# Modulation rows of chunks 4 to 17 as weighted sums on VectorE, in the two projection stages, stored by accumulating transfers

## Chip, cores and metric

The kernel runs on one core of a Trainium2 chip. The metric is the device time of one launch in microseconds; less is better. Five engines work side by side and wait for each other through semaphores: TensorE (PE: matmuls and transposes into PSUM), VectorE (DVE), ScalarE (ACT), GpSimd (POOL; here it only issues transfers) and SyncE (SP; it issues transfers too). All data are float32.

## What is computed

Two transformer-like blocks run one after the other on 512 tokens of width 1024. Each block turns a conditioning vector into rows of shift, scale and gate, the modulation:

```python
# first block
mod = jnp.einsum('bd,de->be', jax.nn.silu(c), w_ada[l]) + b_ada[l]         # 3 x 1024
shift, scale, gate = jnp.split(mod, 3, axis=-1)
h = rms_norm(x, norm_pre[l]) * (1.0 + scale[:, None, :]) + shift[:, None, :]
proj = jnp.einsum('bsd,de->bse', h, w_in[l])
...   # recurrence (RG-LRU), dilated attention, output projection
x = x + gate[:, None, :] * rms_norm(mix, norm_post[l])
# second block
mod = (s_lat @ w_ada[l] + b_ada[l]).reshape(B, N_MOD, 1, D)                # 6 x 1024, latent
mod_c = (s_ctx @ w_ada[l] + b_ada[l]).reshape(N_MOD, 1, 1, D)              # 6 x 1024, context
p_l = modulate(x, norm1_g[l], mod[:, 0], mod[:, 1]) @ w_in[l]
p_c = modulate(ctx, norm1_g[l], mod_c[0], mod_c[1]) @ w_in[l]
...   # pooling, differential attention, RWKV scan, merge, mixture of experts
```

The two weight matrices `w_ada` are cut into 18 chunks of 1024 x 512 (2 MB each): chunks 0 to 5 belong to the first block (0 to 3 are shift and scale, 4 and 5 the gate), 6 to 17 to the second. Chunks 6 to 9 (shift and scale of the second block) are wanted for the latent and for the context vector, chunks 10 to 17 only for the latent one.

## The kernel before

The kernel is written engine by engine: each stage has one function for each engine (`proj1_tensor`, `proj1_vector`, ...), and each engine runs its functions in a fixed order. A wait names the event it needs (`T[...]` from TensorE, `V[...]` from VectorE, `d_...[...]` for a transfer); everything behind it on the same engine waits too. Nothing is reordered at run time. VectorE waits for its own last instruction before each new one.

The stages that matter here, with their place in the trace: the start with the modulation of chunks 0 to 3 (0 to 37 us); the **first projections** (`PROJ1`, 24 tiles of eight 128x512 matmul steps, 37 to 222 us), with the recurrence in them; **attention** (`att_...`, 35 steps over 4 query blocks i and 8 heads h, key width 128(i+1), 222 to 310 us); the **output projection** of the first block (`out1_...`, 8 mix tiles, then norms and transposes, 310 to 391 us); the **second projections** (`TILES2`: pool 0-3, q 0-3, kc/k 0-3 in turn, v 0-5; 391 to 545 us); then differential attention, third projections, the scan, the merge, and from about 1400 us the experts, whose weights stream in.

In attention one step x does on TensorE, in this order: scores of step x+1, transposes of the probabilities of step x-2, a third of a modulation chunk (`ada_tensor`), and the product with V of step x-3. VectorE does bias and row maximum, ScalarE the exponential and the copy of the transposes.

A modulation chunk j from 4 on is computed by `modulation_blocks`: 8 slices k times 4 column groups t, 32 matmuls of `cs[:, k, :]` (128x32, three of its columns hold the vectors) against 128 columns of the weights. `ADA` cuts each chunk into steps of 12, 12 and 8 matmuls; 35 steps stand in the attention loop and the 36th behind it; chunks 16 and 17 stand at the end of `out1_tensor`. `ada_vector(j)` adds the bias and writes `mrow`, and `ada_gpsimd(j)` stores the row to DRAM (`mods1`, `mods2`), from where later stages fetch it. The chunks come through the three 4096-column weight buffers (`MAIN_CHUNKS`, `W`), loaded by SP in one fixed order with all other weights; a load waits until the chunk three places before it is used up. So weight chunk 26, the first of the second projections, waits for chunk 13, the last of the output projection.

`Late` runs short generators beside a row of tiles: each `add` or `step` moves each pending one forward. In the second projections a q or k tile is squared (ACT), summed (`bs` matmul, behind the next tile), rooted (ACT), and on VectorE inverted and scaled (a reciprocal and a `stt`, a scalar_tensor_tensor), then rotated (`rot2` matmul, one more tile later, and three tensor_tensor).

## Time and profile before

| | us |
|---|---|
| median of 3 runs | 1870.52 (1866.34 to 1871.33) |
| span of the profiled execution | 1876.8 |
| TensorE busy | 1717.6 (92%) |
| VectorE busy | 804.7 (43%) |
| ScalarE busy | 518.8 (28%) |
| GpSimd busy | 109.4 (6%) |
| attention, 221.0 to 309.6 | 88.6 |
| output projection with its end, 309.6 to 391.4 | 81.8 |

The page gives the span as the execution's only time; it is 6.3 us above the median of the three timed runs. The row of slices on the page shows TensorE at 9 tenths or more in nearly all of the first 33 of 40 slices, and the DMA row at 9 only from slice 30 on, in the experts. In a timeline row the columns are start, duration, engine, line, operation, destination and source, shapes and count; in brackets stands the idle time before it and what ended it. TensorE's durations of merged rows run from the first start to the last end, and neighbouring rows overlap a little.

### The profile page before, as it was taken

The page shows a single profiled execution, that of the slowest core. Times are in us where ns is not written, and L with a number is a line of the kernel's source. Part 1 is how long each engine was busy: PE and PEld are TensorE (multiplying, and loading weights), DVE is VectorE, ACT ScalarE, POOL GpSimd, SP SyncE. Part 2 cuts the span into 40 slices and gives each one's busy share as a digit, 9 for nine tenths or more (in the row PEclk, how much of TensorE's full clock was granted, in tenths as well). Part 3 has the DMA queues.
Part 4 walks back from the last instruction along what each step waited for, and adds up shares of the span by engine and source line. Part 5 has one row for each costly group of instructions (what it writes and reads, how often), then busy time and mean ns, then how long its engine had stood idle before and what let it go on. Part 6 is the DMA issues. An engine that isn't in the chain of part 4 may idle for free.

```text
span 1876.8 us, 37887 instructions
## 1 busy us (share of the span) xinstructions
PE 1717.6 (92%) x16822; PEld 927.4 (49%) x16822; DVE 804.7 (43%) x1484; ACT 518.8 (28%) x983; POOL 109.4 (6%) x144
## 2 busy tenths in 40 slices
PE   5999999999999999999999999999999977778786
PEld 3444566544546555556667667544454333323332
DVE  3853144656627456355654554344462211222210
ACT  3710254311127422354453341122231110101010
POOL 0000010010000000100000000000001101010100
PEclk8999989999989999999998998899999999999998
DMA  9121376351110030042221210356569999999997
GB/s 396 76 88 47 145 287 247 145 224 69 45 45 1 23 151 0 17 170 82 77 81 50 63 56 24 114 219 221 219 239 398 416 425 415 422 413 425 417 423 279
DMA packets 48360, 359.25 MB, mean 191 GB/s; under 512 B 8325, under 2 KB 8557, under 8 KB 28736
## 3 DMA queue, kind: packets, MB, share of 16 engines
q1 hardware_dynamic: 35792, 311.51, 41.2%
q0 software_dynamic: 12400, 45.27, 7.3%
q8 instruction: 134, 2.20, 0.5%
q14 instruction: 34, 0.28, 0.0%
...
## 4 chain that ended last, share of the span: by engine, by line
PE 74%; DMA 16%; ACT 4%; issue 3%; DVE 2%; POOL 0%; SPq 0%; ACTq 0%; DVEq 0%; POOLq 0%
PE psum L207 71%; DMA arena<-in_w 16%; PE psum L210 3%; ACT arena L204 3%; ACT L204 1%; DVE arena L154 1%; DVE arena L180 0%; DVE arena L164 0%; DVE arena L172 0%; DVE arena L160 0%; POOL arena L141 0%; DMA arena<-in_tok 0%; DVE arena L168 0%; DVE arena L159 0%; POOL out L149 0%
## 5 line engine op out<-in xcount | busy, mean ns | idle before, releaser
L207 PE MATMUL psum<-arena 32*32 32x16 f32 (+12 forms) x16178 | 1638.1, 304 | 145.2 <-DMA arena<-in_w 73.4
L207 PEld LDWEIGHTS psum<-arena 32*32 32x32 f32 (+5 forms) x16178 | 856.0, 135 | 876.3 <-issue 764.7
L204 ACT ACTIVATE arena<-psum 128x512 f32<-128x512 f32 (+5 forms) x334 | 171.4, 513 | 871.2 <-PE psum L207 670.7
L154 DVE TENSOR_TENSOR arena<-arena,psum 128x512 f32<-128x512 f32 (+3 forms) x128 | 64.9, 507 | 402.6 <-PE psum L207 209.2
L154 DVE TENSOR_TENSOR arena<-arena 128x512 f32<-128x512 f32 (+10 forms) x315 | 191.6, 608 | 31.0 <-ACT arena L204 14.7
L204 ACT ACTIVATE arena<-arena 128x512 f32<-128x512 f32 (+10 forms) x254 | 138.8, 546 | 177.7 <-DVE arena L154 41.9
L204 ACT ACTIVATE arena<-psum,arena 128x128 f32<-128x128 f32 (+3 forms) x221 | 111.7, 505 | 275.1 <-PE psum L210 135.5
L154 DVE TENSOR_TENSOR arena<-psum,arena 128x128 f32<-128x128 f32 (+3 forms) x116 | 47.4, 409 | 154.5 <-PE psum L207 141.3
L164 DVE SCALAR_TENSOR_TENSOR arena<-arena 128x512 f32<-128x512 f32 (+7 forms) x162 | 103.5, 639 | 14.5 <-ACT arena L204 8.1
L210 PE MATMUL psum<-arena 128*128 128x128 f32 x644 | 102.6, 291 | 6.1 <-ACT arena L204 3.2
L172 DVE RECIPROCAL arena<-arena 128x1 f32<-128x1 f32 (+4 forms) x71 | 79.1, 1113 | 63.0 <-ACT arena L204 59.2
L210 PEld LDWEIGHTS psum<-arena 128*128 128x128 f32 x644 | 73.6, 146 | 64.3 <-issue 46.0
L164 DVE SCALAR_TENSOR_TENSOR arena<-psum,arena 128x512 f32<-128x512 f32 (+4 forms) x84 | 49.6, 591 | 114.8 <-PE psum L207 111.2
L204 ACT ACT_TABLE_LOAD x68 | 87.2, 1283 | 18.8 <-DMA arena<-gd 11.6
L159 DVE TENSOR_SCALAR arena<-arena 128x32 f32<-128x32 f32 (+10 forms) x126 | 39.8, 316 | 57.7 <-ACT arena L204 52.7
L184 DVE COPY_PREDICATED arena<-arena,psum 128x512 f32<-128x512 uint32 (+1 forms) x60 | 35.9, 598 | 45.4 <-PE psum L207 41.3
L168 DVE COPY arena<-psum 128x512 f32<-128x512 f32 (+4 forms) x53 | 27.8, 525 | 63.2 <-PE psum L210 35.4
L180 DVE TENSOR_REDUCE arena<-psum 128x1 f32<-128x768 f32 x32 | 30.6, 958 | 47.8 <-PE psum L207 46.0
L149 POOL DMA_INDIRECT out<-arena x16 | 25.1, 1566 | 408.6 <-DVE arena L164 139.5
L143 POOL DMA_DIRECT2D arena<-kd x28 | 21.1, 753 | 240.9 <-DVE arena L154 135.3
L143 POOL DMA_DIRECT2D mods<-arena x26 | 14.4, 557 | 312.4 <-DVE arena L154 304.2
L160 DVE TENSOR_SCALAR arena<-psum,arena 128x128 f32<-128x128 f32 x64 | 26.2, 410 | 8.5 <-PE psum L210 5.0
...
## 6 DMA issues: line engine op xcount, KB each, us to landing
...
kd<-arena POOLq DMA_DIRECT2D x2, 1536.0 KB, 11.0
```

Of the source, the lines that this page charges most:

```text
L143: self.e.dma_start(out, in_).then_inc(*signal)
L154: return self.ends(self.e.tensor_tensor(out, a, b, op))
L159: return self.ends(self.e.tensor_scalar(out, a, s1, None, op0))
L160: return self.ends(self.e.tensor_scalar(out, a, s1, s2, op0, op1))
L164: return self.ends(self.e.scalar_tensor_tensor(out=out, in0=a, scalar=s, in1=b, op0=op0, op1=op1))
L168: return self.ends(self.e.tensor_copy(out, a))
L172: return self.ends(self.e.reciprocal(out, a))
L180: return self.ends(self.e.tensor_reduce(out, a, AX, op, negate=negate))
L184: return self.ends(self.e.copy_predicated(out, mask, a))
L204: return self.ends(self.e.activation(out, a, func, **kw))
L207: return self.ends(self.e.matmul(out, lhs, rhs, start=start, stop=stop))
L210: return self.ends(self.e.transpose(out, a, ident))
```

## The change

Chunks 4 to 17 are no longer multiplied on TensorE slice by slice. VectorE forms for each chunk and vector the weighted sum over the 8 slices (each slice 128x512 times a per-partition scalar of `cs`, one `tensor_scalar` and seven `scalar_tensor_tensor`), and TensorE then only sums over partitions: 4 matmuls against a 128x32 matrix with a column of ones (`one_column`), for chunks 6 to 9 twice 4. The bias is not added any more: `mods1` and `mods2` are filled with the bias by two DRAM to DRAM transfers, and the rows are added to them by accumulating transfers.

The weights of these chunks leave the three big buffers. They come in 56 quarters ("parts") of 128x1024 (0.5 MB) into two small buffers (`ada_in`), issued by GpSimd; the load of part n waits until VectorE is done with part n-2. Parts 0 to 23 (chunks 4 to 9) are summed in the first projections, parts 24 to 55 (chunks 10 to 17) in the second. In the attention loop only the 8 matmuls of chunk 9 are left, and in `out1` none. `MAIN_CHUNKS` gets 14 entries shorter, so weight chunk 26 now waits for chunk 11 instead of 13. VectorE's copy `ada_vector(j)` (128x128) and the store stay, spread over the same stages. SP waits for the last store before it loads the first expert chunk, GpSimd before the third projections.

```diff
-MAIN_CHUNKS = [0, 1, 2, 3, 6, 7, 8, 9, 10, 11, 4, 5, *range(14, 24), 12, 13, 24, 25, *range(26, 34), *range(40, 45)]
+MAIN_CHUNKS = [0, 1, 2, 3, 6, 7, 8, 9, 10, 11, 12, 13, *range(26, 34), *range(40, 45)]
...
+                if ("p1", t) in ADA_SUMS:
+                    ada_tensor(ADA_SUMS["p1", t], ALL8)
...
+        ADA_VECTORS = {j: (0,) if j < 6 else (1, 2) if j < 10 else (1,) for j in ADA}
+        ADA_SUMS = {("p1", 12): 4, ("p1", 13): 5, ("p1", 18): 6, ("p1", 20): 7, ("p1", 22): 8, ("att", 2): 9, ("q", 0): 10, ("q", 1): 11,
+                    ("k", 0): 12, ("kc", 2): 13, ("v", 0): 14, ("v", 1): 15, ("v", 3): 16, ("v", 4): 17}
...
+                     ("v", 0): (44, 47), ("v", 1): (47, 50), ("v", 2): (50, 53), ("v", 3): (53, 56)}.items()}
...
+        def ada_load(n):
+
+            j, q = 4 + n // 4, n % 4
+            if n > 1:
+                G.wait_ge(ada_by(n - 2)["part", n - 2])
+            G.dma(ada_in[n % 2].rearrange("p k n -> p (k n)"), T_["w"][ada_chunk(j), :, 1024 * q:1024 * q + 1024], d_aw[n % 2].up(n))
+
+        def ada_part_vector(n):
+
+            j, q = 4 + n // 4, n % 4
+            V.wait_ge(d_aw[n % 2][n])
+            for v in ADA_VECTORS[j]:
+                s = ada_at(j, v)
+                if q == 0 and s > 3:
+                    V.wait_ge(T["ada", ADA_SLOTS[s - 4][0]])
+                for k in range(2):
+                    w, by = ada_in[n % 2][:, k, :], cs[:, 2 * q + k, v:v + 1]
+                    if q == 0 and k == 0:
+                        V.ts(ada_sum[s % 4], w, by, None, ALU.mult)
+                    else:
+                        V.stt(ada_sum[s % 4], w, by, ada_sum[s % 4], ALU.mult, ALU.add)
+            V.then_inc("part", n)
+
+        def ada_tensor(j, ring):
+            T.wait_ge(ada_by(4 * j - 13)["part", 4 * j - 13], *ps.take(ring, "ada", j))
+            last = ADA_VECTORS[j][-1]
+            for v in ADA_VECTORS[j]:
+                for t in range(4):
+                    T.mm(ps["ada", j][32 * t:32 * t + 32, 0:128], one_column(v), ada_sum[ada_at(j, v) % 4][:, c4(t)],
+                         v == ADA_VECTORS[j][0], v == last)
+            T.then_inc("ada", j)
...
-                ada_tensor(*next(steps), MBANK)
+                if ("att", x) in ADA_SUMS:
+                    ada_tensor(ADA_SUMS["att", x], MBANK)
...
+                if before[n, m] in ADA_SUMS:
+                    ada_vector(ADA_SUMS[before[n, m]])
+                for part in ADA_PARTS.get((n, m), ()):
+                    ada_part_vector(part)
...
+            Y.wait_ge(*mods_stored(17))
             Y.dma(EB0, T_["w"][45], WE.count((0, 0)).up("w", (0, 0)))
...
-            G.wait_ge(*end3())
+            G.wait_ge(*end3(), *mods_stored(17))
```

How the change stands in three places. The first is TensorE in attention, at steps with key width 128 and 256 (128x256 and 128x128 on L207 are scores, L210 is the transpose, 128x64 the product with V, 32x128 the modulation). Before:

```order
L207 MATMUL psum<-arena 128x256
L210 MATMUL psum<-arena 128x128 [waits s_dve]
L207 MATMUL psum<-arena 32x128 x8
L207 MATMUL psum<-arena 128x64 [waits s_act]
L207 MATMUL psum<-arena 128x256
L210 MATMUL psum<-arena 128x128 [waits s_dve]
```

And now, from step 2 on (lines are three higher in the changed file):

```order
L213 MATMUL psum<-arena 128x128 [waits s_act]
L210 MATMUL psum<-arena 32x128 x8
L210 MATMUL psum<-arena 128x128 [waits s_dve]
L213 MATMUL psum<-arena 128x128 [waits s_dve,s_act]
L210 MATMUL psum<-arena 128x64 [waits s_act]
L210 MATMUL psum<-arena 128x128 [waits s_dve]
L213 MATMUL psum<-arena 128x128 [waits s_dve]
L210 MATMUL psum<-arena 128x64 [waits s_act]
```

The 32x128 blocks between transpose and V product are gone in every step but one.

The second is TensorE in the v tiles of the second projections. Before (256-column rows are the kc tile's sum; then v 0, the sum of tile k 3, v 1, its rotation, v 2 to 5):

```order
L207 MATMUL psum<-arena 128x512 [waits d_w2]
L207 MATMUL psum<-arena 128x512 x7
L207 MATMUL psum<-arena 128x512 [waits s_act]
L207 MATMUL psum<-arena 128x512 x8
L207 MATMUL psum<-arena 128x512 [waits s_dve]
L207 MATMUL psum<-arena 128x512 x32
```

Now:

```order
L210 MATMUL psum<-arena 128x512 [waits s_act]
L210 MATMUL psum<-arena 32x128 [waits s_dve]
L210 MATMUL psum<-arena 32x128 x3
L210 MATMUL psum<-arena 128x512 x8
L210 MATMUL psum<-arena 128x512 [waits s_dve]
L210 MATMUL psum<-arena 32x128 [waits s_dve]
L210 MATMUL psum<-arena 32x128 x3
L210 MATMUL psum<-arena 128x512 x16
```

Behind v 0 and v 1 (and later v 3 and v 4) stand four short matmuls whose first waits for VectorE, ahead of the next tiles.

The third is VectorE at the same place. Before it had, for tile k 3, the reciprocal, the scaling and the three rotation steps:

```order
L172 RECIPROCAL arena<-arena 128x512 [waits s_dve,s_act]
L164 SCALAR_TENSOR_TENSOR arena<-psum,arena 128x512 [waits s_dve]
L154 TENSOR_TENSOR arena<-arena 128x512 [waits s_dve]
L154 TENSOR_TENSOR arena<-psum,arena 128x512 [waits s_dve,s_pe]
L154 TENSOR_TENSOR arena<-arena 128x512 [waits s_dve]
```

Now (d_aw0 and d_aw1 are the landings of the parts):

```order
L167 SCALAR_TENSOR_TENSOR arena<-psum,arena 128x512 [waits s_dve]
L162 TENSOR_SCALAR arena<-arena 128x512 [waits s_dve,d_aw0]
L167 SCALAR_TENSOR_TENSOR arena<-arena 128x512 [waits s_dve]
L167 SCALAR_TENSOR_TENSOR arena<-arena 128x512 [waits s_dve,d_aw1]
L167 SCALAR_TENSOR_TENSOR arena<-arena 128x512 [waits s_dve]
L167 SCALAR_TENSOR_TENSOR arena<-arena 128x512 [waits s_dve,d_aw0]
L167 SCALAR_TENSOR_TENSOR arena<-arena 128x512 [waits s_dve]
L157 TENSOR_TENSOR arena<-arena 128x512 [waits s_dve]
L157 TENSOR_TENSOR arena<-psum,arena 128x512 [waits s_dve,s_pe]
L157 TENSOR_TENSOR arena<-arena 128x512 [waits s_dve]
L171 COPY arena<-psum 128x128 [waits s_dve,d_mod2]
L167 SCALAR_TENSOR_TENSOR arena<-arena 128x512 [waits s_dve,d_aw1]
```

Parts 44, 45 and 46 stand between the scaling and the rotation of k 3, and part 47, the last of chunk 15, behind the rotation.

## Rows read from the trace of the kernel before

**Rows 1.** The page: span, TensorE, shares of the chain by engine
```profile
span 1876.8 us, 37887 instructions
PE 1717.6 (92%) x16822; PEld 927.4 (49%) x16822; DVE 804.7 (43%) x1484; ACT 518.8 (28%) x983; POOL 109.4 (6%) x144
...
PE 74%; DMA 16%; ACT 4%; issue 3%; DVE 2%; POOL 0%; SPq 0%; ACTq 0%; DVEq 0%; POOLq 0%
```
**Rows 2.** Windows by stage: length; busy PE, PEld, DVE, ACT, POOL; clock, DMA share, GB/s
```profile
221.00:309.60 88.60, 87.13 (x1011) 56.97 (x1010) 44.85 (x95) 46.99 (x112) 11.06 (x20) 0.94 0.73 277
309.60:371.90 62.30, 62.30 (x236) 30.78 (x237) 32.63 (x40) 18.04 (x35) 2.75 (x5) 1.00 0.47 182
371.90:391.40 19.50, 14.88 (x170) 10.52 (x168) 8.70 (x12) 5.28 (x10) 3.06 (x5) 0.82 0.85 338
391.40:508.50 117.10, 115.60 (x317) 58.86 (x318) 70.97 (x73) 18.18 (x30) 2.20 (x4) 1.00 0.23 84
```
**Rows 3.** Groups by form, TensorE, 224 to 309.5 us: busy us, mean ns | idle before
```profile
L207 PE MATMUL psum<-arena 128*32 128x128 f32 x672 | 26.3, 287 | 0.4 <-DVE arena L154 0.4
```
**Rows 4.** Timeline in attention: two early steps, a table load, an idle, the last modulation block
```profile
235.58 1.64 PE L207 MATMUL psum<-arena 128*32 128x128 f32 x20
237.41 1.85 PE L207 MATMUL psum<-arena 128*32 128x128 f32 x28
...
247.95 1.28 ACT L204 ACT_TABLE_LOAD   x1
...
250.38 2.35 PE L207 MATMUL psum<-arena 128*128 128x64 f32 x6 [1.11 <-ACT arena L204]
...
309.58 0.65 PE L207 MATMUL psum<-arena 128*32 128x128 f32 x16
```
**Rows 5.** Windows of 4 us (columns as in rows 2; the granted clock is third from the end)
```profile
252.00:256.00 4.00, 4.00 (x33) 2.45 (x32) 1.11 (x2) 1.28 (x5) 0.00 (x0) 0.50 0.97 415
256.00:260.00 4.00, 4.00 (x31) 2.14 (x32) 0.00 (x0) 0.38 (x1) 0.00 (x0) 0.50 0.01 4
...
380.00:384.00 4.00, 2.80 (x5) 1.59 (x6) 2.69 (x4) 1.04 (x3) 0.00 (x0) 0.56 1.03 442
```
**Rows 6.** Timeline at the end of the output projection
```profile
371.91 1.91 PE L210 MATMUL psum<-arena 128*128 128x128 f32 x16
...
375.31 1.06 ACT L204 ACTIVATE arena<-arena 128x1024 f32<-128x1024 f32 x1 [0.66 <-DVE arena L168]
...
381.20 8.44 PE L207 MATMUL psum<-arena 128*128 128x384 f32 x16 [3.75 <-DMA arena<-in_w]
...
382.63 1.23 DVE L154 TENSOR_TENSOR arena<-arena 128x1024 f32<-128x1024 f32 x1
...
391.39 14.04 PE L207 MATMUL psum<-arena 128*128 128x128 f32 x44 [0.88 <-DVE arena L168]
```
**Rows 7.** Groups by form, VectorE, 36 to 560 us
```profile
L164 DVE SCALAR_TENSOR_TENSOR arena<-arena 128x512 f32<-128x512 f32 x27 | 19.9, 736 | 0.9
```
**Rows 8.** Transfers issued by GpSimd: count, KB each, median us from issue to landing
```profile
fd<-arena POOLq DMA_DIRECT2D x4, 512.0 KB, 3.0
...
arena<-in_ropes POOLq DMA_DIRECT2D x1, 1536.0 KB, 6.8
...
arena<-in_norm_post POOLq DMA_DIRECT2D x1, 512.0 KB, 8.9
```
**Rows 9.** Timeline at the end of the first projections, VectorE
```profile
215.75 0.69 DVE L154 TENSOR_TENSOR arena<-arena,psum 128x512 f32<-128x512 f32 x1 [6.18 <-ACT arena L204]
...
223.44 0.29 DVE L164 SCALAR_TENSOR_TENSOR arena<-psum,arena 128x128 f32<-128x128 f32 x1
```
**Rows 10.** Timeline in the v tiles
```profile
504.62 0.48 DVE L164 SCALAR_TENSOR_TENSOR arena<-psum,arena 128x256 f32<-128x256 f32 x1
...
513.58 0.75 DVE L164 SCALAR_TENSOR_TENSOR arena<-psum,arena 128x512 f32<-128x512 f32 x1
...
516.33 0.60 ACT L204 ACTIVATE arena<-psum 128x512 f32<-128x512 f32 x1 [6.18 <-PE psum L207]
517.19 0.69 DVE L154 TENSOR_TENSOR arena<-psum,arena 128x512 f32<-128x512 f32 x1 [2.14 <-PE psum L207]
```

113 lines of the change are left out of this document (61 added, 52 removed).

## The prediction, made before the changed kernel ran

> **What bounds the kernel now.** I read the page first: span, busy shares, the chain by engine. TensorE is busy 92% of 1876.8 us, and the chain that ended last is TensorE for 74%, a weight transfer for 16% [rows 1]. The transfers are those of the experts, from about 1500 us on; they start when buffers come free, so what the early stages save moves them forward whole, and I count an early microsecond as one of the end. Then the windows by stage: TensorE is busy 87.1 of 88.6 us in attention, all of the eight mix tiles' 62.3, only 14.9 of the 19.5 behind them, and 115.6 of 117.1 in the second projections up to tile k 3, while VectorE has work for 44.9, 32.6, 8.7 and 71.0 [rows 2]. So TensorE's own list of work is the bound, save at the end of the output projection, and VectorE has room almost everywhere; the question is whether it has it where its results are wanted.
>
> **Attention: minus 23.5, plus 0.5.** 672 records of modulation matmuls are busy 26.3 us there [rows 3]; each matmul is two records, 12 chunks are 768, and the last block of 16 adds 0.65 [rows 4]: 27 us at most. That counts each block's fill and drain. A row with 8 more records is 0.21 us longer (1.64 against 1.85 [rows 4]), 0.026 each: 768 of them are 20.2 us at least. The blocks stand between other matmuls and hide part of their ends, so I take the middle, 23.5. Chunk 9's 16 records give back 0.5.
>
> **Attention: plus 2.5 for ScalarE, plus 1 for the clock.** The blocks cover waits. After query block 0 two table loads, of which one is shown (1.28), hold ScalarE up, and TensorE idles 1.11 [rows 4]. A step there takes 1.83 with a block of 16 (from start to start of the two rows) and 2.05 with one of 24; it falls to 1.4 with the same loads in it, so this idle grows by up to 1.3, and two like places (after query blocks 1 and 2) may open by 0.6 each: 2.5, between 0 and 5. Otherwise TensorE still bounds: ScalarE is busy 47.0 for 35 steps [rows 2], 1.34 a step, and TensorE has 1.9 to 2.0 left. The granted clock is 0.50 in both windows after that idle, that is 1.2 GHz instead of 2.4 [rows 5]. The same steps will see it again; I add 1 us, and leave two more such dips to a rival. Sum of attention: -19.5.
>
> **First projections: plus 2.5.** Chunks 4 to 8 leave 8 groups of 4 matmuls (8 records) between tiles. At 0.026 a record each is 0.21; with some switch, 0.25: 2.0 on TensorE, uncovered, because it never idles there. Parts 0 to 23 cost VectorE 16 instructions for chunks 4 and 5 together and 64 for 6 to 9. At 0.736 [rows 7] plus a gap of 0.04, a part is 1.56 for one vector, 3.1 for two. Where it counts is the last seven tiles: 2 parts of 3.1 plus the gate's 0.69 is 6.9 per tile, and a tile takes 6.87 (0.69 busy plus 6.18 idle [rows 9]). VectorE thus goes from nearly idle to full, but it starts these parts ahead of TensorE, as the tiles before (chunk 10) need nothing from it. My walk gives part 23 done near 223.8 and the first attention bias at 225.2, against 223.44 [rows 9] plus 2.0 of TensorE's shift: no delay. That needs each load to land in time: of two buffers, a load begins when its forerunner's sum ends and must land within one other part, 3.1, or VectorE waits the rest. For the landing of 512 KB the rows give 3.0 (a store) and 8.9 (while SP's queue filled the engines); 6.8 for 1536 KB [rows 8] less 2.5 for 1024 KB at 415 GB/s [rows 5] is 4.3. I take 3.4, nearer to the store, which has the size and found idle engines as the parts will, plus 0.4 for the two wake-ups: 3.8. The first tile with a single wait (a raw copy behind parts 6 and 7, which follow the long norm) costs 0.3. Sum +2.5 with rounding up; bounds +2 and, at a landing of 4.3, +4. The Trainium skill (DMA: Bandwidth & Descriptors, Anatomy of one DMA — SWDGE (gpsimd) path) fits 2.0 us plus bytes over 436 GB/s to one such transfer: 3.2 us here by estimate, and the sum would be 1 us less by it; no row here is a 512 KB load alone.
>
> **End of the output projection: minus 5.4, plus 1.9.** Before, the transposes of tile 3 end at 373.8, the modulation of chunks 16 and 17 follows, TensorE idles 3.75 for weight chunk 26, runs the first pool tile's 384 columns at half clock in 8.44, and goes on at 391.39 [rows 6]. Now the blocks are gone, and chunk 26 is free to load from the end of the first projections. What is late next is the norm of the last 128 tokens: squares at 375.31, VectorE's last add ends at 383.86 [rows 6], then 8 transposes (16 take 1.91) and a copy (its wait is the 0.88): the second projections resume at about 386.0. That is 5.4 earlier, not the 3.7 + 3.75 + 3.2 that the idle and the blocks suggest. The pool columns (three quarters of a tile's 6.87, 5.2 at full clock) fill 375.3 to 380.5, after which TensorE idles 3.4; before, after 3.75 idle, the clock was 0.56 [rows 5]. Half clock on what follows costs 1.9. Bounds -5.4 and -2. Sum: -3.5.
>
> **Second projections: plus 2.0, plus 0.5.** Chunks 10 to 17 are 8 groups of 4 matmuls, 0.25 each. The parts here are of one vector, 1.56. VectorE is busy 71.0 of 117.1 us [rows 2] and gets 20 parts more, 31 us: 87%. In a q tile it waits 2.1 for the rotation (as at 517.19 [rows 10]), and one part fits in. Where a part and its reader come close (chunk 13) I add 0.5.
>
> **The v tiles: plus 8.4, plus 2.** Here the order bites. TensorE's sum of chunk 15 stands behind v 1 and waits for part 47; VectorE does part 47 only after the rotation of tile k 3. Tile v 1 ends at 516.2 (ScalarE's copy begins at 516.33), the rotation's matmul at 517.1 (VectorE reads it at 517.19) [rows 10]. VectorE ends the scaling of k 3 at 514.33 [rows 10]; part 44 to 516.0, 45 to 517.5 (both landed: part 43 was done at 506.7, 1.56 after the row at 504.62), 46 is issued when 44 ends and lands 3.8 later at 519.8, done 521.4; three rotation steps to 523.5, the copy of chunk 14 to 523.9, part 47 to 525.5. TensorE stands from 517.1 to 525.5: 8.4. Were the loads instant, it would be 6.1; with a landing of 4.3, 9.3. Before, nothing waited here. The halved clock after so long an idle costs some 2 (as in rows 5), between 0 and 3.4. Behind that, parts 48 to 55 come at one per 2.7 us; part 51 is done at 536 and 55 at 547, TensorE wants them at 541 and 548 or so: no further stall, but little room. VectorE then issues chunk 17's copy, GpSimd its store and the pooled branch's store queued behind it, for which ScalarE waits at the start of differential attention; it lands near the end of v 5, and ScalarE has nothing to do before the first scores and their maximum: 0.
>
> Stores, the bias copies and the waits of SP and GpSimd on the last store cost nothing: SP reaches its wait only after a load that the third projections release, 20 us later.
>
> **Sum.** -19.5 + 2.5 - 3.5 + 2.5 + 10.4 = -7.6. Against the profiled 1876.8 that is 1869.2; the timed median lies 6.3 lower, so I take it off there: 1870.5 - 7.6, about **1863**.
>
> **Rivals.**
> A, *attention is held up by others*: without the filler the small matmuls of blocks 0 and 1 leave ScalarE's chain or the clock as the bound. For it: a mere 1.11 us of idle was followed by two windows at 0.50 [rows 4, 5], and with narrow keys TensorE's step falls to ScalarE's 1.3. Against: TensorE keeps 1.9 to 2.0 a step on average. Two more dips of 8 us at half clock, 4 each: +8, 1871.
> B, *slower than before: the loads of parts land late*. Every microsecond beyond 3.8 costs one per pair of parts: 6 pairs in the last tiles of the first projections and some 3 more where the v tiles wait, about 9 us. So it decides from 1.5 us more, a landing of about 5: the gain is gone and 1876 passed; at 5.5, 1880. For: the one 512 KB load in the rows took 8.9. Against: SP's stream ran beside that one, and now has nothing to load in that stretch but two chunks. The Trainium skill has a rule to the same end (SBUF — State Buffer, Who interferes with whom): GpSimd writes the descriptors of its transfers through a port pair shared with VectorE, and an exclusive lock keeps it out. It names plain copies and tensor_scalar from SBUF as what takes it, and says that two-input instructions block only GpSimd's reads; by that, 14 first instructions of 0.45 would matter and 126 would not. Were all of them to lock it, each load would wait out a part.
> C, *more comes free*: attention gives the whole 27, clock dips do not come, the stall in the v tiles is 6: -15, 1855.
> D, the modulation blocks are gone but TensorE stalls for other parts that I walked past (VectorE is 90% full in two stretches): a few us each, 1870.
>
> **How the numbers follow.** About 0.3% (5.6 us) is what can be told from no change. The forecast 0.50 with its own range 1857 to 1869, A 0.15, D 0.07, C 0.14, B 0.14. The forecast's bounds are the terms' (-4 and +5 on attention, 1.5 elsewhere, not all at once). The range runs from within C to the lower edge of B, 1852 to 1878, and leaves out 0.2. Faster by more than 5.6: C, and two thirds to three quarters of the forecast, 0.50; slower: B, 0.14; between, 0.36.
>
> **What the profile would show.** Attention of about 69 us, with TensorE busy nearly throughout, idle after block 0 of about 2, and one clock dip. TensorE back at the pool tiles 14 us after the last mix tile (19.5 before). One idle of about 8 us on TensorE in the v tiles, ended by VectorE. Landings of the parts at 3 to 4 us, and VectorE busy without waits on them before attention. Wrong would be: idles on TensorE at the start of attention (B), a clock below 0.9 in its first 30 us (A), or no stall behind v 1 (my walk of VectorE's order).

## The result: slower by 2.5%, where a small gain was predicted

| kernel | median of the timed runs, us | range, us | ratio to before (95% interval) |
|---|---|---|---|
| before | 1870.92 | 1866.34 to 1876.81 | |
| changed | 1918.43 | 1914.09 to 1924.13 | 1.0255 (1.0224 to 1.0285) |

The change costs 47.5 us where the prediction had a gain of 7.6; the range 1852 to 1878 does not hold the time, and the sign is wrong. The profiled execution of the changed kernel has a span of 1912.3 us, 35.5 more than the one of before. (The profiled execution of before was the longest of its four, that of the changed kernel the shortest of its four, so the profiles show 12 us less than the medians.) The ratios in this document are worked out from the single executions of both kernels, mostly without those far above the fastest, so they are not exactly the quotients of the medians.

The page of the changed kernel: span, the two rows of slices that matter (40 equal slices of 47.8 us), the chain by engine, and the loads of parts.

```profile
span 1912.3 us, 36605 instructions
...
PE   5999999989988889999999999999999978777786
...
PEclk9999955999988999999998999999999999999998
...
PE 64%; DMA 18%; issue 9%; DVE 6%; ACT 3%; POOL 0%; SPq 0%; DVEq 0%; POOLq 0%; ACTq 0%
...
arena<-in_w POOLq DMA_DIRECT2D x56, 512.0 KB, 4.4
```

The answer to [rows 1] is not in the shares but in the PEclk row: two 5s in the sixth and seventh slice (239 to 335 us), which is attention. And 56 loads of 512 KB took 4.4 us in the median, not 3.4.

The windows by stage (length; busy PE, PEld, DVE, ACT, POOL; clock, DMA share, GB/s), which answer to [rows 2]: attention, the end of the output projection, the second projections up to 530 us, and the v tiles with TensorE's stand behind v 1.

```profile
230.20:329.60 99.40, 94.75 (x319) 63.71 (x319) 44.57 (x89) 46.95 (x112) 5.11 (x7) 0.54 0.07 22
...
384.50:403.60 19.10, 13.56 (x53) 7.71 (x52) 12.32 (x15) 5.57 (x11) 0.00 (x0) 0.97 0.53 206
403.60:530.00 126.40, 123.99 (x363) 62.41 (x364) 102.26 (x118) 19.46 (x32) 15.89 (x27) 0.98 0.45 153
530.00:569.00 39.00, 30.16 (x79) 12.55 (x77) 22.36 (x31) 2.10 (x4) 7.20 (x12) 0.87 0.43 135
```

Attention has a third of the matmul records that it had (319 against 1011), yet TensorE is busy for 94.75 us instead of 87.13, and the granted clock is 0.54 instead of 0.94. The timeline shows it step by step (start, duration, what it is, idle before it in brackets). The rows are the start of attention, a step of query block 0 and the end of block 3 with the first mix tiles:

```profile
233.78 0.48 PE L210 MATMUL psum<-arena 64*128 64x128 f32 x2 [3.59 <-DVE arena L171]
...
243.28 0.47 PE L213 MATMUL psum<-arena 128*128 128x128 f32 x1
243.55 1.68 PE L210 MATMUL psum<-arena 128*128 128x64 f32 x4
245.16 0.47 PE L213 MATMUL psum<-arena 128*128 128x128 f32 x1
...
331.55 20.84 PE L210 MATMUL psum<-arena 128*128 128x512 f32 x48 [0.88 <-DVE arena L157]
```

Such a step takes 1.88 us (243.28 to 245.16), nearly as long as the steps of 1.83 and 2.05 of before with their modulation blocks in them [rows 4]; the first few, with scores of 128 columns beside them and not 256, take 1.45. A single transpose takes 0.47. The same in windows of 4 us:

```profile
236.00:240.00 4.00, 4.00 (x21) 2.77 (x14) 2.03 (x7) 2.75 (x11) 2.83 (x4) 0.50 0.14 31
...
320.00:324.00 4.00, 4.00 (x17) 3.26 (x17) 1.38 (x2) 1.41 (x3) 0.00 (x0) 0.50 0.00 0
324.00:328.00 4.00, 4.00 (x24) 4.00 (x22) 0.36 (x1) 1.19 (x2) 0.00 (x0) 0.57 0.00 0
328.00:332.00 4.00, 3.12 (x25) 2.84 (x25) 1.79 (x4) 0.60 (x1) 0.00 (x0) 1.00 0.02 4
```

Before, two windows were at 0.50 and the clock came back by 264 us [rows 5]. Now 22 windows in a row are at 0.50, with TensorE busy 3.73 to 4.00 us of 4 in each.

Where the 35.5 us came in, from the same events in both timelines (time of after minus time of before, and how much each stage added):

| up to | before | after | later by | stage adds | predicted |
|---|---|---|---|---|---|
| first bias of attention on VectorE | 223.44 | 233.86 | 10.4 | +10.4 | +2.5 |
| first mix tile of the output projection | 313.8 | 331.55 | 17.7 | +7.3 | -19.5 |
| end of the mix tiles' transposes | 373.8 | 391.5 | 17.7 | 0 | 0 |
| TensorE back after the last norm | 391.39 | 403.62 | 12.2 | -5.5 | -3.5 |
| rotation of tile k 3 done on TensorE | 517.1 | 536.1 | 19.0 | +6.8 | +2.5 |
| first scores of differential attention | 545.40 | 577.58 | 32.2 | +13.1 | +10.4 |
| its last transposes | 649.47 | 680.48 | 31.0 | -1.2 | 0 |
| tiles of the third projections | 742.35 | 783.46 | 41.1 | +10.1 | 0 |
| end | 1876.8 | 1912.3 | 35.5 | -5.6 | 0 |

(313.8 is the end of the row of 25.10 us at 309.58, 334.68, less three mix tiles, 20.84 as in the row at 331.55.) Three stages are far from the prediction: attention by 27 us, the start of the third projections by 10, the first projections by 8. The last line is spread over the scan, and differs between executions of one kernel.

The new stand ahead of the third projections, from all engines' timelines:

```profile
680.48 0.60 PE L213 MATMUL psum<-arena 128*128 128x128 f32 x4
...
682.13 0.56 POOL L143 DMA_DIRECT2D brd<-arena  x1 [109.88 <-DVE arena L171]
686.39 0.19 DVE L157 TENSOR_TENSOR arena<-arena 128x32 f32<-128x32 f32 x1 [4.57 <-DMA brd<-arena]
...
688.55 1.23 ACT L207 ACTIVATE arena<-psum 128x512 f32<-128x512 f32 x2 [15.21 <-DVE arena L179]
...
689.20 10.99 PE L210 MATMUL psum<-arena 128*128 128x512 f32 x21 [8.12 <-ACT arena L207]
```

GpSimd stores and VectorE waits 4.57 for it, clears two buffers, and only then does ScalarE empty two PSUM banks, at 688.55. TensorE stands 8.12 us for that. In the kernel before the same chain ran (ScalarE's row there is at 657.51) and TensorE worked on beside it from 649.90, without a wait.

### The profile page after: what moved, and what is told of

It reads as the page before. It is cut to its first block, busy times and chain, and to the rows that moved or that the text cites. A ratio compares the mean times of both kernels' runs of the same rounds, so it can differ in the third digit from the quotient of the medians.

```text
span 1912.3 us, 36605 instructions
## 1 busy us (share of the span) xinstructions
PE 1729.5 (90%) x16070; PEld 929.9 (49%) x16070; DVE 908.2 (47%) x1629; ACT 518.5 (27%) x983; POOL 142.0 (7%) x193
## 4 chain that ended last, share of the span: by engine, by line
PE 64%; DMA 18%; issue 9%; DVE 6%; ACT 3%; POOL 0%; SPq 0%; DVEq 0%; POOLq 0%; ACTq 0%
PE psum L210 61%; DMA arena<-in_w 18%; PE psum L213 3%; DVE arena L167 3%; ACT arena L207 2%; DVE arena L157 1%; DVE arena L175 1%; ACT L207 1%; DVE arena L171 0%; DMA brd<-arena 0%; DVE arena L163 0%; POOL arena L141 0%; DVE arena L162 0%; DMA arena<-in_tok 0%; DVE arena L179 0%
## 5 line engine op out<-in xcount | busy, mean ns | idle before, releaser
L210 PE MATMUL psum<-arena 32*32 32x16 f32 (+8 forms) x15426 | 1644.5, 308 | 165.8 <-DMA arena<-in_w 67.8
L210 PEld LDWEIGHTS psum<-arena 32*32 32x32 f32 (+4 forms) x15426 | 855.0, 138 | 894.4 <-issue 761.6
L207 ACT ACTIVATE arena<-psum 128x512 f32<-128x512 f32 (+5 forms) x334 | 171.2, 512 | 907.7 <-PE psum L210 695.8
L167 DVE SCALAR_TENSOR_TENSOR arena<-arena 128x512 f32<-128x512 f32 (+6 forms) x288 | 198.2, 688 | 51.0 <-DMA arena<-in_w 31.3
L157 DVE TENSOR_TENSOR arena<-arena 128x512 f32<-128x512 f32 (+10 forms) x315 | 191.6, 608 | 32.2 <-ACT arena L207 15.9
L207 ACT ACTIVATE arena<-arena 128x512 f32<-128x512 f32 (+10 forms) x254 | 138.8, 546 | 175.9 <-DVE arena L157 40.0
L207 ACT ACTIVATE arena<-psum,arena 128x128 f32<-128x128 f32 (+3 forms) x221 | 111.5, 505 | 276.3 <-PE psum L213 141.1
L213 PE MATMUL psum<-arena 128*128 128x128 f32 x644 | 111.1, 308 | 9.0 <-DVE arena L157 4.9
L213 PEld LDWEIGHTS psum<-arena 128*128 128x128 f32 x644 | 78.8, 155 | 79.1 <-issue 57.6
L157 DVE TENSOR_TENSOR arena<-psum,arena 128x128 f32<-128x128 f32 (+3 forms) x102 | 43.3, 425 | 108.8 <-PE psum L210 95.8
L162 DVE TENSOR_SCALAR arena<-arena 128x512 f32<-128x512 f32 (+8 forms) x144 | 48.6, 337 | 71.0 <-ACT arena L207 63.4
L171 DVE COPY arena<-psum 128x512 f32<-128x512 f32 (+4 forms) x67 | 31.9, 476 | 61.5 <-PE psum L213 31.0
L143 POOL DMA_DIRECT2D arena<-in_w x58 | 31.4, 543 | 332.6 <-DVE arena L167 302.7
```

Of the source, the lines that this page charges most:

```text
L143: self.e.dma_start(out, in_).then_inc(*signal)
L157: return self.ends(self.e.tensor_tensor(out, a, b, op))
L162: return self.ends(self.e.tensor_scalar(out, a, s1, None, op0))
L167: return self.ends(self.e.scalar_tensor_tensor(out=out, in0=a, scalar=s, in1=b, op0=op0, op1=op1))
L171: return self.ends(self.e.tensor_copy(out, a))
L207: return self.ends(self.e.activation(out, a, func, **kw))
```

## Experiments

All of them are edits of the changed kernel or of the kernel before; "before" in the ratios is the kernel before, timed on the same chip beside them. The diffs are shortened. Microseconds "less" or "more than the changed kernel" are against its 1918.43, which was timed on another occasion with an interval of 1.0224 to 1.0285: all edits of it but e2, e12 and e15 have intervals that overlap this one, so for them the readings rest on the stages in the traces and not on the difference of the medians. Where a profile is quoted it is of one execution.

**The ring of PSUM banks.** `ps.take(ALL8, ...)` hands out eight banks in turn and makes the taker wait until the last user's result is read. The change moved 11 more takers into that ring.

```diff
 def proj3_tensor():
...
+            ps.turn[ALL8] += 5
             late = Late()
```

> The changed kernel, with one edit that does no work: five turns of the ring of eight PSUM banks are skipped ahead of the third projections. The change took 13 turns of that ring for its sums where the kernel before took 2, 11 more, which leaves the ring 3 banks further on at this place; 5 more make it 16, a whole number of rounds. Theory (ring): in the changed kernel TensorE stands 8.1 us at 681 because the ring there comes to banks that ScalarE empties only after a chain of a copy, a transfer and two memsets; the stand is not in the kernel before. With the old phase it is gone and the time is 8 to 10 us lower than the changed kernel, about 1909. Rival: the stand comes from the chain itself, late for another reason, and the third projections find it again whatever the bank: no change, 1918.

Measured: 1906.51 us, ratio 1.0209 (1.0176 to 1.0242), 12 us less than the changed kernel. TensorE's row after the transposes now has no wait:

```profile
680.46 0.60 PE L213 MATMUL psum<-arena 128*128 128x128 f32 x4
680.90 19.50 PE L210 MATMUL psum<-arena 128*128 128x512 f32 x53
```

So a stage that the diff does not touch lost 10 us (8.12 of stand, the rest halved clock behind it), through a counter modulo 8. That the stand goes with the turn of the ring is shown by the trace; of the 12 us in the medians, 2 are not accounted for.

**The clock in attention.** Five kernels: filler in the loop, the blocks taken from the kernel before alone, dense matmuls ahead of the loop, both, and dense matmuls in the loop.

```diff
+                if n: T.wait_ge(*ps.take(MBANK, "fill", x))            # e2, e6: n = (12, 12, 8)[x % 3]
+                for b in range(n):
+                    T.mm(ps["fill", x][32 * (b % 4):32 * (b % 4) + 32, 0:128], cs[:, b % 8, :], ident, True, True)
+                    # e12 instead, one a step: T.mm(ps["fill", x], ident, HT[:, x % 8, :], True, True)
...
+            for k in range(8):                                         # e5, e6, e12, ahead of scores(0)
+                T.mm(ps["bridge"], ident, HT[:, k % 8, :], True, True)
```

> The changed kernel, with useless work added to TensorE in attention: in each of the 35 steps 12, 12 or 8 matmuls of the modulation's form (128x32 against 128 columns) into a PSUM bank that nobody reads, 372 in all, nearly what the change took out (384). Clock theory: the blocks were what kept the granted clock at 1.0 in attention; without them it is 0.50 from 236 to 325 us, which costs more than the blocks' 23.5 us of work. With the filler the clock is back at about 0.9 to 0.95 and attention takes about 90 us instead of 97.7, so that the kernel is some 8 us faster by doing more: about 1910. Rival (something else slows attention, for example the later start or VectorE): the clock stays at 0.5, the filler adds its own 20 us at least at the full clock, 40 at half: 1940 or more.

Measured: 1957.29 (1922.05 to 1960.92), ratio 1.0472 (1.0446 to 1.0499): the rival's number. The six executions differ: 1922.05 and 1940.51 with a mean granted clock of 0.951 and 0.943, the other four at 1956 to 1961 with 0.926 to 0.932. Even the shortest is 2.8% over the kernel before. It is the profiled one, with a span of 1920.2. In windows of 6 us:

```profile
282.00:288.00 6.00, 6.00 (x58) 3.70 (x56) 0.80 (x2) 1.48 (x4) 0.00 (x0) 0.50 0.01 3
288.00:294.00 6.00, 6.00 (x51) 3.88 (x47) 3.12 (x6) 1.84 (x6) 0.00 (x0) 0.81 0.00 0
294.00:300.00 6.00, 6.00 (x84) 3.89 (x78) 4.16 (x7) 2.29 (x6) 0.00 (x0) 1.00 0.01 3
```

The clock is at 0.50 from the start of the loop, then comes back and stays. In this execution the blocks lifted a fallen clock only after some 50 us; in the kernel before the clock was back 10 us after its fall, with the same blocks in the loop [rows 5]. The miss pointed at the 3.6 us of idle ahead of the loop, which the kernel before does not have.

> The kernel before, with the modulation of chunks 4 to 15 cut to 4 matmuls a chunk instead of 32, at the third step of each; the loads, the waits on them, the copies and the stores stay where they are. Left out: 28 of 32 matmuls of these chunks, so the modulation rows are not those of the reference. No other part of the change is in it. Clock theory: attention falls to half clock as in the changed kernel and takes 95 us or more; the time is about 1877 to 1880, no gain from 336 matmuls less. The terms of my prediction: attention shorter by 20, 1850. Between them lies a kernel in which the clock falls for a part of attention only, 1860.

Measured: 1883.05 (1866.43 to 1895.61), ratio 1.0040 (1.0010 to 1.0071). 336 matmuls fewer in 35 steps make the kernel before no faster, rather slower. Its profile has the clock at 0.50 all through attention, and there is no new VectorE work and no new load in it:

```profile
222.00:228.00 6.00, 3.75 (x21) 2.52 (x21) 4.13 (x14) 4.66 (x16) 0.59 (x1) 0.84 1.03 380
228.00:234.00 6.00, 6.00 (x24) 3.60 (x23) 2.29 (x7) 2.57 (x11) 0.55 (x1) 0.50 0.98 418
324.00:330.00 6.00, 6.00 (x35) 5.53 (x34) 1.42 (x4) 0.60 (x1) 1.10 (x2) 0.50 0.78 312
```

This is the longest of the seven executions, but the fall is not its alone: the mean granted clock of the other six is 0.938 to 0.950, that of the ten executions of the kernel before beside them 0.959 to 0.965. What this run does not tell apart is the thin loop and the idle at its start. TensorE waits 2.04 us for ScalarE ahead of the first transpose (busy 3.75 in the first row), where the kernel before has blocks to do and no idle. So the expectation that follows is not right in saying that no idle stood there.

> The changed kernel, with eight useless 128x512 matmuls on TensorE between the first projections and the first scores, where it stood idle for 3.6 us (230.2 to 233.8); their result goes to a PSUM bank that nobody reads. The attention loop stays without blocks. Theory 'idle at the start': the clock fell because of this idle alone, and with it covered the loop runs at 2.4 GHz and takes about 70 us: the time falls by 20 or more, to 1895. Theory 'loop': the loop's own small matmuls and waits bring the clock down whatever stands ahead of them, as in e3_bare, where no such idle stood: 0.50 again within some us of the start, and the time is that of the changed kernel, 1915 to 1920.

> The changed kernel with both additions: the eight dense matmuls ahead of attention, and in each of its steps the filler of 12, 12 or 8 matmuls of the modulation's form (e2_fill). Theory: the blocks hold a full clock but bring a halved one back only slowly (e2_fill had 0.50 until 288 us, then 1.00). With no idle ahead of them the clock stays at 1.0 from the start, as in the kernel before, and attention takes 88 to 92 us: about 1910, 8 less than the changed kernel although TensorE has 372 matmuls more. Rival: the clock falls anyway and the filler costs its 35 to 45 us: 1950.

Measured: e5 1928.93, ratio 1.0295 (1.0246 to 1.0345); e6 1912.09, ratio 1.0246 (1.0179 to 1.0313). First e5, then e6, at the start of the loop:

```profile
234.00:240.00 6.00, 4.60 (x35) 2.34 (x33) 2.60 (x9) 1.78 (x8) 1.98 (x4) 1.00 0.29 85
240.00:246.00 6.00, 5.91 (x23) 4.02 (x21) 2.97 (x10) 3.83 (x15) 2.29 (x4) 0.62 0.54 180
```
```profile
240.00:246.00 6.00, 5.59 (x98) 3.89 (x94) 2.60 (x9) 2.44 (x10) 2.83 (x4) 1.00 0.36 118
...
264.00:270.00 6.00, 4.90 (x57) 2.92 (x56) 2.31 (x5) 4.39 (x12) 0.00 (x0) 1.00 0.01 3
```

And the first transpose of e5:

```profile
237.89 0.33 PE L213 MATMUL psum<-arena 128*128 128x128 f32 x1 [1.18 <-ACT arena L207]
```

With a full clock at the start and no blocks, the clock falls within the first steps (e5). With the blocks it stays at 1.00 to the end of attention, even over an idle of 1.1 us (4.90 of 6.00). Attention takes 87.6 us in e6 (237.0 to 324.58) against 97.7 in the changed kernel, with 372 matmuls more. Theory "loop" is borne out against the idle of 3.6 us: without blocks the loop loses the clock, with that idle covered. Whether its thin steps do it or the shorter idle that the missing blocks leave open at its start (1.18 in e5, none there in e6) is not separated by any run. The bridge itself delays the start, from 233.86 to 236.7; that is 2.8 of the 10.5 us by which e5 is above the changed kernel, and the rest is not placed.

> The changed kernel with the eight dense matmuls ahead of attention (e5_bridge) and, in each of the 35 steps, one useless 128x512 matmul instead of the filler of 12, 12 and 8 small ones: 0.43 us of work a step, 15 us in all, against 20 to 24. It asks whether it is the number of small blocks that holds the clock or the share of time in which TensorE streams columns. Theory 'columns': one matmul of 512 columns keeps the clock at 1.0 and attention takes 80 to 85 us, 1903 to 1907 in all. Theory 'blocks': the clock falls as in e5_bridge and attention takes 97 plus up to 30 us: 1945.

Measured: 1902.88, ratio 1.0160 (1.0122 to 1.0198), the best repair of attention. The clock is 1.00 in every window from 216 to 330, and attention takes 87.1 (236.90 to 323.98). Behind the same bridge, 35 matmuls of 512 columns hold the clock as well as the 372 small ones of e6; so it is not the number of instructions. 15 us of the 87 are that filler (35 times 0.43), which leaves an estimated 72 for the real work at full clock. The prediction had 90.4 less 19.5, that is 71. It had the time of the loop at full clock nearly right and the clock that it runs at wrong. My estimate of 80 to 85 for this stage was 2 too low.

**The dose.** The kernel before with fewer slices multiplied in attention.

> The kernel before, with half of the modulation blocks in attention: of the eight slices of chunks 4 to 15 only 0, 2, 4 and 7 are multiplied, 16 matmuls a chunk instead of 32 (8, 4 and 4 in the three steps). Left out: the other half of these products, so the rows are not those of the reference. Loads, waits and stores are as before. It is the dose between the kernel before (32, clock 0.94) and e3_bare (4, clock 0.50 from 228 to 330 us). Theory 'the blocks hold the clock, all or nothing': it falls here too and the loop is slow with half its blocks: 1880 to 1890. Theory 'any steady filler is enough': the clock stays up and 192 matmuls less save half of 20 to 27 us: 1859.

> The kernel before with three quarters of the blocks: slices 0, 1, 3, 4, 6 and 7 of chunks 4 to 15, 24 matmuls a chunk (8 in each step). Left out: slices 2 and 5, so the rows are not those of the reference. Where the clock stays up: 96 matmuls less save 5 to 7 us, 1865. Where it falls as in e3_bare: 1885. If the clock can go either way near this dose, the timed runs scatter over both.

Measured: half 1899.73 (1875.60 to 1912.92), ratio 1.0114 (1.0072 to 1.0156); three quarters 1863.95 (1853.37 to 1891.52), ratio 0.9968 (0.9931 to 1.0005). Both scatter over 37 us, where the kernel before lies within 21. The shortest execution of half a dose is the profiled one; the clock falls at the idle behind query block 0 and stays down for seven windows:

```profile
246.00:252.00 6.00, 3.97 (x24) 2.31 (x24) 2.77 (x6) 3.90 (x11) 1.10 (x2) 0.62 1.01 427
252.00:258.00 6.00, 6.00 (x33) 3.69 (x25) 0.69 (x1) 1.03 (x3) 0.00 (x0) 0.50 0.25 101
...
288.00:294.00 6.00, 6.00 (x31) 3.63 (x32) 1.67 (x3) 1.30 (x3) 1.10 (x2) 0.50 0.85 309
294.00:300.00 6.00, 6.00 (x41) 3.67 (x39) 3.65 (x6) 2.31 (x6) 0.00 (x0) 0.90 0.10 41
```

So it is no switch at one dose. In these three profiles the less filler, the longer the fall lasts: one window of 6 us at 0.50 with three quarters, seven with half, the whole stage with an eighth. They are single executions, one of them the shortest and one the longest of its kind, but the mean granted clocks of all executions go the same way: 0.957 to 0.970 in the kernel before, then 0.944 to 0.969, 0.931 to 0.955 and 0.935 to 0.950, the last two hardly apart. The idle behind query block 0 grows too, from 1.11 to 1.54 and 2.03, so thinner steps and longer idle come together here. Half a dose costs more than an eighth (e3), probably because it has more work at the same halved clock.

**The landings.** Without loads, with a third buffer, and with the parts earlier.

```diff
-            if n > 1:
-                G.wait_ge(ada_by(n - 2)["part", n - 2])                # e8: return here, no load; no wait on d_aw
+            if n > 2:                                                  # e16: three buffers up to part 23
+                back = 3 if n < 24 else 2
+                G.wait_ge(ada_by(n - back)["part", n - back])
```

> The changed kernel without the loads of parts 2 to 55 and without VectorE's waits on them: all sums are made from the first two parts. Left out: the weights of these parts, so the modulation rows are not those of the reference; all instructions of VectorE and TensorE stay. It says what the landings cost. By the prediction's walk the stand behind tile v 1 falls from 8.4 to 6.1, and the first projections lose 1 or 2 us: 3 to 5 less than the changed kernel, 1914. If VectorE's 31 us of waits on landings all counted, 15 or more less. If none did, 1918.

> The changed kernel with a third buffer for the parts of the first projections (0 to 23), in columns that the change had left unused; a load waits for the part three places before it. Theory: it is two buffers against parts of 1.6 us that make the landing of 4.3 us count; with three the waits of 3.1 and 3.3 us on VectorE at 124 and 135 us go, with them TensorE's idle of 3.1 at 149.6 and its halved clock behind, and attention starts 6 to 8 us earlier, as without loads (e8, 9 us earlier): 1911. Rival: the transfers themselves are slow one behind the other, and the waits only move: 1917.

Measured: e8 1905.48, ratio 1.0196 (1.0157 to 1.0236), 13 less than the changed kernel; e16 1912.08, ratio 1.0234 (1.0198 to 1.0270), 6 less. VectorE in the changed kernel at 130 to 153 us, then the row of TensorE that waits for it:

```profile
131.22 0.75 DVE L167 SCALAR_TENSOR_TENSOR arena<-arena 128x512 f32<-128x512 f32 x1
135.30 1.54 DVE L167 SCALAR_TENSOR_TENSOR arena<-arena 128x512 f32<-128x512 f32 x2 [3.33 <-DMA arena<-in_w]
...
143.30 6.39 DVE L167 SCALAR_TENSOR_TENSOR arena<-arena 128x512 f32<-128x512 f32 x8
...
151.98 0.69 DVE L171 COPY arena<-psum 128x512 f32<-128x512 f32 x1
...
152.72 7.56 PE L210 MATMUL psum<-arena 128*128 128x512 f32 x20 [3.09 <-DVE arena L171]
```

Its load was issued at 131.00, so it landed 4.3 later. The parts of chunks 4 and 5 are of one vector, 1.56 us, the first of a chunk a little less. A load is issued 0.4 after the part two places before it ends. So VectorE waits 0.4 plus the 4.3 or so, less the one part that it has to work on meanwhile: 3.15 at 124 and 3.33 at 135. The long reciprocal and the parts behind it then push the raw copy of a tile to 151.98 (146.33 before), and TensorE stands 3.09 us. In e16 that copy is at 148.85, TensorE does not wait, and the first attention bias is at 226.74, 7.1 earlier than in the changed kernel; in e8 at 224.92, 8.9 earlier. So it is the two buffers, as the theory had it; the 6 us in the medians alone would not show it. Behind v 1 the stand is 5.35 without loads (8.49 with them; the prediction gave 6.1 and 8.4).

> The changed kernel, with parts 9 to 23 one tile earlier in the first projections and the sums of chunks 6, 7 and 8 two tiles earlier, so that VectorE has no part behind tile 22. Theory: the last tiles were too full for VectorE (parts of 3.1 us twice, loads that land 0.7 late, groups on TensorE of 0.77), so that attention began 10.4 us later than before instead of 2.5; 3.6 of it is TensorE's idle ahead of the first scores. With the parts earlier that idle is gone: 3 to 4 us less, 1914. If the clock in attention hangs on that idle, as one theory of the bridge has it, 20 less. Rival: the parts are late everywhere, waits appear in front of the earlier sums, and nothing is won.

Measured: 1923.48, ratio 1.0292 (1.0253 to 1.0330), not faster than the changed kernel. The rival was right: TensorE waits for the sums instead, the longest here:

```profile
214.84 25.12 PE L210 MATMUL psum<-arena 128*32 128x128 f32 x72 [5.38 <-DVE arena L167]
```

**The stand behind v 1.** The sum of chunk 15 one tile later.

```diff
-                    ... ("v", 0): 14, ("v", 1): 15, ("v", 3): 16, ("v", 4): 17}
+                    ... ("v", 0): 14, ("v", 2): 15, ("v", 3): 16, ("v", 4): 17}
```

> The changed kernel, with TensorE's sum of chunk 15 behind tile v 2 instead of v 1; nothing else is moved. Its last part is done on VectorE at the same time as before. Theory of the prediction: the stand of 8.5 us behind v 1 goes down by one tile, 6.9, to 1.6 or less, and with it the halved clock behind it: 8 to 9 us less than the changed kernel, about 1910. Rival: VectorE is full, and the stand moves to the sums of chunks 16 and 17, whose parts come one tile later relative to TensorE: half of it or more comes back, 1914 to 1918.

Measured: 1918.05, ratio 1.0261 (1.0236 to 1.0286): no change. In the changed kernel there is one stand, of 8.49, then 0.66; here there are three:

```profile
544.63 24.03 PE L210 MATMUL psum<-arena 128*32 128x128 f32 x64 [8.49 <-DVE arena L167]
```
```profile
544.63 7.49 PE L210 MATMUL psum<-arena 128*32 128x128 f32 x24 [1.60 <-DVE arena L167]
556.92 10.42 PE L210 MATMUL psum<-arena 128*32 128x128 f32 x24 [4.80 <-DVE arena L167]
570.67 9.51 PE L210 MATMUL psum<-arena 128*32 128x128 f32 x22 [3.34 <-DVE arena L167]
```

1.60, 4.80 and 3.34 are 9.7, with the clock halved twice behind them. VectorE's parts come at their own pace, and a sum placed later only moves where TensorE meets it. The rival was right.

**Do the causes add up?**

> The changed kernel with the remedies together: the ring turned by 5 ahead of the third projections (e1: -12), no loads of parts 2 to 55 (e8: -13; left out are the weights of these parts, so the rows are not those of the reference), the eight dense matmuls ahead of attention and one dense matmul in each of its steps (e12: -15.5). If the three causes are separate and whole, they add: 1918 - 12 - 13 - 15.5 = 1878. Left then against the kernel before: 5 us of stand behind v 1, the groups on TensorE and the dense filler, against the blocks. If they overlap (the landings and the clock both act on the start of attention): 1885 or more.

Measured: 1885.98, ratio 1.0086 (1.0054 to 1.0118), 8 above the sum of the single gains. The overlap is at the start of attention. Without loads VectorE is ready earlier, but the bridge still takes its 3.5 us: the first bias is at 231.91 here and at 224.92 in e8, 7.0 later. In the changed kernel the bridge delayed it by 2.8 only. That is 4 of the 8; the rest I can't place.

**Smaller changes that might win.** Chunks 16 and 17 alone, then 12 to 17, as sums on VectorE in the second projections, one part to a tile (two in v 0 to v 3); chunks 4 to 11 stay in the first 24 steps of attention.

```diff
+        BLOCKS = [(j, q) for j in range(4, 12) for q in range(3)]
+        ADA_SLOTS = [(j, 1) for j in range(12, 18)]
+        ADA_SUMS = {("q", 0): 12, ("kc", 0): 13, ("kc", 2): 14, ("v", 1): 15, ("v", 3): 16, ("v", 4): 17}
...
+            ps.turn[ALL8] += 4
```

> A smaller change, complete and equal to the reference in what it computes: only chunks 16 and 17 are weighted sums on VectorE, their 8 parts one to a tile in the second projections (q 1 to kc 2), where VectorE has room; chunks 4 to 15 stay as matmul blocks in attention as before, with the loads through the big buffers. The ring of banks has as many turns as before. By the prediction's own terms that the changed kernel bore out: the end of the output projection gives 5.5 us (blocks of 16 and 17 gone, weight chunk 26 early), two groups of 4 matmuls cost 0.45 each, attention keeps its clock: 4 to 5 us faster than before, 1866. Rival: something of the new loads or sums stalls TensorE in the q and k tiles: no gain, 1871 or more.

> A version between the two, complete: chunks 4 to 11 stay as blocks in the first 24 steps of attention (narrow keys, query blocks 0 to 2), chunks 12 to 17 are weighted sums on VectorE in the second projections, one part to a tile and two in the v tiles; no sums in the first projections, and the ring of banks is brought back to the phase of the kernel before. Sum: attention loses 128 matmuls in its wide steps, 8 us; the end of the output projection gives 5.5; six groups on TensorE cost 0.45 each, 2.7; no stand behind v 1, since chunk 15 is complete before it. If the wide steps hold the clock at 1.0 by themselves: 10 us faster than before, 1861. If the clock falls there: these 11 steps take up to twice as long, 10 to 15 us back, 1872 to 1876.

> e13_six_chunks with one useless 128x512 matmul (0.43 us) in each of the last 11 steps of attention, where it has no blocks. If the clock of e13_six_chunks falls in the wide steps, this holds it and the kernel is 5 to 10 us faster than that one, about 1866. If it holds there anyway, this only adds 4 us.

Measured: e11 1870.23, ratio 0.9987 (0.9965 to 1.0009); e13 1868.19, 0.9982 (0.9959 to 1.0005); e14 1875.46, 1.0018 (0.9993 to 1.0043). e11 and e13 cannot be told from before; the 4 to 5 us expected of e11 are not seen. In e13 the wide steps hold the clock until an idle of 1.6 us, behind query block 2, and TensorE leaves that at 0.51:

```profile
288.00:294.00 6.00, 5.56 (x33) 3.60 (x31) 4.80 (x7) 3.04 (x7) 0.00 (x0) 1.00 0.00 0
294.00:300.00 6.00, 4.39 (x23) 2.57 (x22) 4.38 (x8) 5.61 (x10) 0.00 (x0) 0.92 0.02 4
300.00:306.00 6.00, 6.00 (x31) 6.00 (x31) 0.10 (x1) 3.19 (x7) 0.00 (x0) 0.51 0.00 0
```

e14's dense matmuls hold it (1.00 to the end) and seem to cost more than they save: they stand in all 11 steps, 4.7 us, and the fall in e13 lasts 6 us only.

The last two runs cut the 32 matmuls of a chunk differently over its three steps, so that the step with the idle behind query block 0 gets the large part.

```diff
-ADA_K = (range(3), range(3, 6), range(6, 8))
+ADA_K = (range(2), range(2, 4), range(4, 8))
```

> e13_six_chunks with the 32 matmuls of a chunk cut into 8, 8 and 16 instead of 12, 12 and 8. The step in which TensorE waits 1.1 us for ScalarE behind query block 0 is one with the third part of a chunk: it has then 8 matmuls more, 0.65 us, and the idle shrinks to 0.45. If that idle is what brings the clock down to 0.50 between 250 and 262 us, the dip is gone in most executions and the time falls by 3 to 4 us, 1865. Rival: the clock falls by the thin stretch as a whole, steps of 8 matmuls make it worse, and the time is that of e13 or more, 1868 to 1880.

> The kernel before with the same cut of each chunk, 8, 8 and 16 matmuls, and no other edit. The work is the same. If the idle behind query block 0 starts the dip: 3 to 4 us faster than before, 1867. If steps with 8 matmuls are too thin to hold the clock (e9_half had 8, 4 and 4): slower, 1875 to 1890, and the runs scatter.

Measured: e17 1864.92 (1859.63 to 1870.91), ratio 0.9961 (0.9941 to 0.9982); e18 1869.78, ratio 0.9990 (0.9971 to 1.0010). e17 is the one version whose interval lies below 1, by a gain of 0.4%. Of eighteen versions tried, one so near the edge can be chance, and nothing repeats it; its interval also overlaps that of e13. Its runs lie within 11 us. The idle behind query block 0 is 0.66 us in its profile (0.67 in e18's, 1.11 before), and the clock does not fall there (it still falls in the wide steps, behind the same idle of 1.6 us as in e13):

```profile
248.00:252.00 4.00, 3.34 (x57) 2.21 (x56) 2.05 (x6) 3.52 (x10) 1.71 (x2) 1.00 0.76 242
252.00:256.00 4.00, 4.00 (x42) 2.60 (x34) 1.14 (x3) 1.15 (x4) 0.00 (x0) 1.00 0.92 382
```

e18 has no dip in its profile either, but a gain for it alone is not shown.

## Why the prediction was wrong, point by point

The forecast failed at the term "plus 1 for the clock" in attention, which measured 26; a term of 10 us at the third projections that the prediction did not have, and one of 2.5 in the first projections that measured 10.4, make up most of the rest.

**What bounds the kernel.** Right as far as it went: TensorE's own list of work is the bound in attention. But the time of that list is work divided by clock, and I took the clock of the kernel before as given.

**Attention, "minus 23.5" and "plus 1 for the clock".** The term that failed is the second. The blocks' work did go (e12: 72 us left at full clock, 71 predicted), and what made 97.7 of it is the halved clock, which cutting the blocks alone brings about (e3). I wrote that "the same steps will see it again", one dip of 1 us; it lasted the whole stage and cost 26, an estimate: the 97.7 measured less 72. The hint stood in [rows 4] and [rows 5]: 1.11 us of idle was followed by two windows at 0.50 even with the blocks around it. I read that as the price of an idle; it was a sign of how near the loop is to losing the clock, and with fewer blocks it stayed down longer (e10, e9, e3). Rival A named the right cause with the wrong size (+8, "two more dips of 8 us") and got 0.15.

That 72 meets 71 is in part luck. The 90.4 from which the 71 is reckoned holds about 5 us of half clock (windows at 0.85, 0.50, 0.50 and 0.87 between 248 and 264 us), which e12 does not have. And the small blocks, net of the waits that they cover, cost 15.6 us at full clock (e6's 87.6 less 72, for 372 of them), where "minus 23.5, plus 2.5" makes 21. Two errors of about 5 us cancel.

**"Plus 2.5 for ScalarE".** Not seen at half clock, where TensorE is the slow one: ScalarE's longest hold in the narrow steps is 0.8. With half the blocks and the clock still up (e9), the idle behind query block 0 is 2.03 instead of 1.11, so the growth by up to 1.3 is real there. In e12 TensorE waits 1.0 for ScalarE in all, with the dense filler covering part of it.

**First projections, "plus 2.5", measured +10.4.** Two terms of this are mis-sized and one was missed. The eight groups take 3.0 us instead of 2.0. The landing was 4.3 to 4.4, and 4.7 to 4.8 from the end of the part two places before, instead of 3.8; "at a landing of 4.3, +4" was my own upper bound, and it was too low, because I charged the landing to the last seven tiles only. The miss is in chunks 4 and 5: their parts last 1.56, and two buffers cannot hide 4.3 behind that. The raw copy for which I put 0.3 came late and cost 3.09 and 1.9 of halved clock (the tiles' matmuls are busy 186.9 instead of 185.0). "My walk gives part 23 done near 223.8": it was done at 232.5, of which TensorE's own delay is 7.6. Rival B had this mechanism, but with its lever in the last tiles; e16 shows that a third buffer takes back 7.1 of the 7.9.

**End of the output projection, "minus 5.4, plus 1.9", and second projections, "plus 2.0, plus 0.5".** The resume is 5.5 earlier, TensorE's idle for the norm is 3.8 (3.4 predicted), and it comes back 13.8 us after the last mix tile (14 predicted). The halved clock came behind it, within the second projections, and cost 3.7 instead of 1.9 (16 records of transposes 3.8 instead of 2.0 us, the tiles' matmuls 109.8 instead of 107.9). Five groups take 2.1 (0.42 each, 0.25 predicted), the wait for part 39 0.8 (0.5 predicted). Together +1.3 against -1.0.

**The v tiles, "plus 8.4, plus 2".** The stand is 8.49. That walk through VectorE's queue had the order and the mechanism right; that its number is right to a tenth is luck. Part 46 landed 4.6 after part 44's end (538.76 against 534.13) and not 3.8, so that VectorE ended part 47 11.8 after the scaling of k 3 instead of 11.2, and TensorE came to its wait 3.4 behind that scaling instead of 2.8. By its own line "with a landing of 4.3, 9.3" the walk would have been 0.8 too long; without loads it was so too (6.1 against 5.35). The stage as a whole added 13.1: besides the stand another wait of 0.66, 2.8 of halved clock instead of 2 (65 records busy 30.9 instead of 28.1), and 1.5 for its three groups of 4 matmuls, which the prediction had booked at 0.25 each in the term before. What surprised is e4: the sum of chunk 15 placed later does not save the stand.

**Elsewhere: nothing predicted, +10.1 at the third projections.** "TensorE stalls for other parts that I walked past" (D, 0.07, 1870) had no such mechanism in it. The change moves 11 takers from a bank of their own into a shared ring, and I looked at where their work goes, not at the ring.

**Chances.** "Slower" had 0.14, all on one mechanism. Three came, of 26, 10 and 8 us beyond my terms, each unlikely in my reckoning; the range was made from the bounds of my terms, and the causes lay outside the terms. Two of the prediction's three signs of being wrong were there in the first profile: the idle of 3.59 at the start of attention, and a clock below 0.9 in its first 30 us. In its argument on rival B, the 14 first instructions of a chunk's sum are 18, since chunks 6 to 9 have two vectors, and last 0.49 each; nothing in the sum rests on them.
